# Turning queries and keys with VectorE and the sync queue in place of TensorE

## The reference, cut to what matters

```python
q = (_rmsnorm(c_q, q_norm_g) @ w_uq).reshape(Bsz, S, MLA_H, MLA_QK)
...
dq = _rope(_rmsnorm(d_q.reshape(Bsz, S, DIL_H, DIL_HD), dil_q_g[l]), positions)
dk = _rope(_rmsnorm(d_k.reshape(Bsz, S, DIL_H, DIL_HD), dil_k_g[l]), positions)
y_d = _dilated_attention(dq, dk, d_v.reshape(Bsz, S, DIL_H, DIL_HD)) * jax.nn.silu(g_d)
y = jnp.concatenate([y_a, y_b, y_c, y_d], axis=-1).astype(x.dtype)
x = x + y @ w_out[l]
```

## Time and profile before

| | us |
|---|---|
| three timed runs | 823.65, 824.35, 824.37 |
| median | 824.35 |
| the profiled execution | 823.59 |
| its span, first to last instruction | 821.61 |
| PE busy | 816.4 (99%) |
| VectorE busy | 625.2 (76%) |
| ScalarE busy | 478.2 (58%) |

### The profile page before, as it was taken

How to read it: one execution, slowest core, us unless ns; L and a number is a source line. 1 busy time by engine, 2 the same in 40 slices (tenths; PEclk the granted TensorE clock), 3 DMA queues, 4 the chain that set the end, 5 groups by cost and what they waited for, 6 DMA issues and landing times.

```text
span 821.6 us, 11397 instructions
## 1 busy us (share of the span) xinstructions
PE 816.4 (99%) x4244; PEld 693.0 (84%) x4244; DVE 625.2 (76%) x1118; ACT 478.2 (58%) x788; POOL 54.1 (7%) x64
## 2 busy tenths in 40 slices
PE   9999999999999999999999999999999999999998
PEld 5888888999888888888888888889998888888886
DVE  6678799876886986678965977979769868965542
ACT  6665534777865566433556464357697665654341
POOL 7200000200200000000000000002012000000000
PEclk9999999999999999999999999999999999999999
DMA  9956634566654445655576655457657433456653
GB/s 333 352 204 211 192 129 153 145 208 180 208 176 154 129 132 201 191 191 187 177 253 184 200 161 169 129 147 200 191 173 220 164 129 129 158 177 210 196 189 119
DMA packets 47607, 150.98 MB, mean 184 GB/s; under 512 B 5504, under 2 KB 6192, under 8 KB 47552
## 3 DMA queue, kind: packets, MB, share of 16 engines
q1 hardware_dynamic: 47040, 149.98, 57.0%
q10 hardware_dynamic: 320, 0.21, 0.1%
q0 software_dynamic: 192, 0.07, 0.1%
HBM read 148.13 MB, written 2.11 MB: 183 GB/s over the span
## 4 chain that ended last, share of the span: by engine, by line
PE 91%; DVE 7%; issue 2%; DMA 1%; SPq 0%; ACT 0%; DVEq 0%
PE gemm L665 26%; PE gemm L674 26%; PE gemm L666 26%; DVE arena L1323 3%; DVE w_lo L1354 2%; PE pairs L857 1%; PE pairs L846 1%; PE pairs L833 1%; PE pairs L838 1%; PE pairs L834 1%; PE pairs L795 1%; PE pairs L731 1%; DVE arena L1433 1%; PE pairs L872 1%; DMA u<-in_xT_dram 1%
## 5 line engine op out<-in xcount | busy, mean ns | idle before, releaser
L1354 DVE TENSOR_TENSOR w_lo<-raw,w_hi 128x1024 fp32r<-128x1024 f32 (+2 forms) x295 | 324.7, 1110 | 144.4 <-ACT w_hi L997 142.9
L665 PE MATMUL gemm<-w_hi,a_hi 128*128 128x512 f32 (+1 forms) x1144 | 421.6, 374 | 0.0
L666 PE MATMUL gemm<-w_hi,a_lo 128*128 128x512 f32 (+1 forms) x1144 | 414.4, 368 | 0.0
L997 ACT ACTIVATE w_hi<-raw 128x1024 fp32r<-128x1024 f32 (+2 forms) x295 | 281.0, 967 | 191.4 <-PE gemm L674 136.1
L674 PE MATMUL gemm<-w_lo,a_hi 128*128 128x512 f32 (+1 forms) x1144 | 281.8, 368 | 0.3
L665 PEld LDWEIGHTS gemm<-w_hi,a_hi 128*128 128x128 f32 x1144 | 215.2, 188 | 35.6 <-issue 1.3
L666 PEld LDWEIGHTS gemm<-w_hi,a_lo 128*128 128x128 f32 x1144 | 215.3, 188 | 33.0
L674 PEld LDWEIGHTS gemm<-w_lo,a_hi 128*128 128x128 f32 x1144 | 203.2, 188 | 36.6 <-DVE w_lo L1354 2.0
L573 POOL TENSOR_TENSOR st<-st,powers 128x4 f32<-128x4 f32 (+2 forms) x8 | 8.6, 1074 | 431.5 <-ACT arena L1075 213.4
L1195 ACT ACTIVATE arena<-arena,st 128x128 f32<-128x128 f32 (+1 forms) x32 | 13.1, 444 | 35.4 <-DVE st L1616 35.4
L1027 ACT ACTIVATE u<-gemm,st 128x512 f32<-128x512 f32 (+1 forms) x40 | 22.1, 605 | 18.8 <-PE gemm L674 18.8
(11 more groups left out here) (200 smaller groups left out, 639.0 us busy)
## 6 DMA issues: line engine op xcount, KB each, us to landing
raw<-in_weights_dram SPq DMA_DIRECT2D x225, 512.0 KB, 4.1
raw<-in_weights_dram SPq DMA_DIRECT2D x64, 278.0 KB, 3.1
raw<-in_weights_dram SPq DMA_DIRECT2D x6, 384.0 KB, 3.4
x<-in_x_dram SPq DMA_DIRECT2D x4, 512.0 KB, 6.2
o<-ssd_rows SPq DMA_DIRECT2D x8, 256.0 KB, 4.9
param_rows<-in_params_dram SPq DMA_DIRECT2D x2, 904.0 KB, 7.1
u<-in_xT_dram SPq DMA_DIRECT2D x3, 512.0 KB, 8.1
out_dram<-x SPq DMA_DIRECT2D x3, 512.0 KB, 6.4
```

What stands on the lines that cost most here:

```text
L665: pe.matmul(acc_t[t], a_hi[:, k, tok[t]], hi, start=k == 0, stop=False)
L666: pe.matmul(acc_t[t], a_lo[:, k, tok[t]], hi, start=False, stop=False)
L997: A_(w_hi[:, g % SPLIT, 0:c], raw[:, g % RAW, 0:c], ACT.Copy).then_inc(hi_done, 1)
L1354: TT(w_lo[:, g % SPLIT, 0:c], raw[:, g % RAW, 0:c], w_hi[:, g % SPLIT, 0:c].bitcast(F32), ALU.subtract).then_inc(split_done, 1)
```

## The change

Four of the five jobs leave PE and PSUM; `mla rT` stays. In their place each of the four turns has three steps. `turn_squares` on DVE transposes squares of 32x32 in place of their partitions, 128 partitions at a time, in two instructions of 512 elements, into a buffer (`fold`, for the dilated keys a piece of the arena). The sync queue then moves the squares across the partitions in 16 DMAs of 32 partitions by 256 elements from SBUF to SBUF (`across`). ACT copies the result into the layout that the scores read, as it did from PSUM. `HEADS_AT` gives for each turn the unit of the DVE step, of the DMAs and of the copy. Added waits: SP for the squares; ACT for the DMAs; DVE, ahead of a turn, for the DMAs of the turn before that used the same buffer; and `y_turn` now waits for the copy `dil kT` in place of PE's `mla rT`. `y_turn` starts one unit later.

```diff
-          "mla kv 1": KV_AT, "ssd Y": 76, "ssd yb": 81, "mla qT": 85, "mla kT": 86, "mla rT": 87, "mla S 0": 89, "mla PT 0": 92,
-          "mla S 1": 93, "mla O 0": 94, "dil qT": 95, "mla PT 1": 96, "dil kT": 97, "mla O 1": 98, "dil S 0": 99,
+          "mla kv 1": KV_AT, "ssd Y": 76, "ssd yb": 81, "mla rT": 87, "mla S 0": 89, "mla PT 0": 92,
+          "mla S 1": 93, "mla O 0": 94, "mla PT 1": 96, "mla O 1": 98, "dil S 0": 99,
...
-Y_TURN = {1: 97, 0: 101}
+Y_TURN = {1: 98, 0: 102}
...
+        SQUARES = {"mla q": A(3072, 1024), "mla k": A(4096, 1024), "dil q": u[:, 0, 0:1024], "dil k": u[:, 1, 0:1024]}
+        FOLD = {"mla q": fold, "mla k": fold, "dil q": fold, "dil k": A(6656, 1024)}
+
+        HEADS_AT = {"mla q": (79, 84, 86), "mla k": (85, 90, 88), "dil q": (90, 95, 94), "dil k": (92, 97, 96)}
...
+            def across(to, source, arrived):
+
+                for i in range(4):
+                    for f in range(4):
+                        sp.dma_start(to[32 * f:32 * f + 32, i * S:(i + 1) * S], source[32 * i:32 * i + 32, f * S:(f + 1) * S]).then_inc(arrived, 16)
...
+                    for name in HEADS_AT:
+                        if n == HEADS_AT[name][1]:
+                            sp.wait_ge(*reached("dve", l)(f"{name} squares"))
+                            across(SQUARES[name], FOLD[name], squares_in[name])
...
                 def heads_T(name, dst):
-                    act_.wait_ge(*pe(name))
-                    A_(dst, pair_of(name).rearrange("p b (k s) -> p (b k) s", k=2), ACT.Copy).then_inc(*signal("act", name))
+
+                    act_.wait_ge(squares_in[name], 16 * 16 * (l + 1))
+                    act_.wait_ge(*dve("mla rope" if name[:3] == "mla" else "dil rope 1"))
+                    A_(dst.rearrange("p h (t i a) -> p i (h t) a", t=T, i=4), SQUARES[name].rearrange("p (i c a) -> p i c a", i=4, a=32), ACT.Copy).then_inc(*signal("act", name + "T"))
...
+            def turn_squares(to, rows):
+
+
+                to = to.rearrange("p (f k t a) -> p t k f a", f=4, k=4, t=T)
+                for t in range(T):
+                    last = v.transpose(to[:, t], rows[:, t].rearrange("p k (f b) -> p k f b", f=4))
+                return last
...
                     v.wait_ge(*me(f"y {j}"))
-                    v.wait_ge(*pe("mla rT"))
+
+                    v.wait_ge(*act("dil kT"))
...
+                def head_squares(name):
+
+                    m, i = name[:3], "qk".index(name[4])
+                    if name == "mla k":
+                        v.wait_ge(squares_in["mla q"], 16 * 16 * (l + 1))
+                    if name == "mla q" and l:
+                        v.wait_ge(squares_in["dil q"], 16 * 16 * l)
+                    if name == "dil q":
+                        v.wait_ge(squares_in["mla k"], 16 * 16 * (l + 1))
+                    v.wait_ge(*me(f"mla n {i} 1" if m == "mla" else f"dil rope {i}"))
+                    heads = (mqk if m == "mla" else dqk)[:, :, 4 * i:4 * i + 4, 0:P]
+                    turn_squares(FOLD[name], heads).then_inc(*sig(f"{name} squares"))
```

More of the change, by code:

```diff
@@ L230 @@
         "gla level 6, gla level 7, gla out, ssd cum, ssd gcol, ssd CB, ssd xs, "
-        "mla cT, ssd Y, ssd yb, mla qT, mla kT, mla rT, "
-        "mla S 0, mla PT 0, mla S 1, mla O 0, dil qT, mla PT 1, dil kT, mla O 1, dil S 0, dil PT 0, dil S 1, dil O 0, "
+        "mla cT, ssd Y, ssd yb, mla rT, "
+        "mla S 0, mla PT 0, mla S 1, mla O 0, mla PT 1, mla O 1, dil S 0, dil PT 0, dil S 1, dil O 0, "
         "dil PT 1, dil O 1, yT 2, yT 3",
@@ L239 @@
         "evac 8, mla kv 0, mla kv 1, mla rs 1 sum, dil rs 0 sum, evac 9, dil rs 1 sum, ssd y, mla qT, mla kT, evac 10, "
-        "mla rT, mla P 0, ssd rs sum, mla PT 0, mla P 1, evac 11, dil qT, mla PT 1, dil kT, dil P 0, dil PT 0, "
+        "mla rT, mla P 0, dil qT, ssd rs sum, mla PT 0, dil kT, mla P 1, evac 11, mla PT 1, dil P 0, dil PT 0, "
         "evac 12, dil P 1, dil PT 1, yT 0, yT 1, yT 2, evac 13, yT 3",
@@ L247 @@
         "conv 0 3, conv 0 4, conv 0 5, ssd CB, mla cn, ssd E 0, ssd xdt, mla cT, ssd E 1, ssd M 0, ssd M 1, "
-        "mla n 0 0, mla n 0 1, ssd yT, mla n 1 0, mla n 1 1, mla rope products, mla rope, dil n 0 0, dil n 0 1, "
-        "dil n 1 0, dil n 1 1, dil rope 0 products, dil rope 0, dil rope 1 products, dil rope 1, mla max 0, "
[1 row of a table removed]
+        "mla n 0 0, mla n 0 1, ssd yT, mla q squares, mla n 1 0, mla n 1 1, mla rope products, mla rope, mla k squares, dil n 0 0, dil n 0 1, "
+        "dil n 1 0, dil n 1 1, dil rope 0 products, dil rope 0, dil q squares, dil rope 1 products, dil rope 1, dil k squares, mla max 0, "
[1 row of a table added]
         "dil nmax 0, dil P 0, y turn 0, dil max 1, dil nmax 1, dil P 1, dil ri 0, dil O 0, y 2, yT 0, dil ri 1, dil O 1, yT 1, "
@@ L303, in build @@
         eps, minus_half, log_scale = powers[:, 0:8], powers[:, 8:16], powers[:, 16:17]
+        fold = sb("fold", [P, S * 4])
         st = sb("st", [P, 161])
@@ L428, in build @@
         warm = sem("warm")
+        squares_in = {name: sem(name.replace(" ", "_") + "_squares_in") for name in HEADS_AT}
         setup_chain = sem("setup_chain")
@@ L886, in values, with mla_rT @@
                     last.then_inc(*signal("pe", f"{m} O {i}"))
[L888 removed]
+                def mla_rT():
                     pe.wait_ge(*dve("mla rope"))
[L890 to L895 removed]
                     rr = mrr.rearrange("p t (a b) d -> p t a (b d)", b=2)
@@ L900, in _ @@
                        "gla out": gla_out, "ssd xs": ssd_xs, "ssd cum": ssd_cum, "ssd gcol": ssd_gcol, "ssd CB": ssd_CB, "ssd Y": ssd_Y, "ssd yb": ssd_yb, "mla cT": mla_cT,
-                       "mla qT": mla_qT, "mla kT": mla_kT, "mla rT": mla_rT}
+                       "mla rT": mla_rT}
                 def stages(n):
@@ L1183, in head_sums, with mla_rT @@
                     last.then_inc(*signal("act", f"{m} rs {i} sum"))
+                def mla_rT():
+                    act_.wait_ge(*pe("mla rT"))
+                    A_(mrT.rearrange("p a b s -> p (a b) s"), pair_of("mla rT").rearrange("p b (k s) -> p (b k) s", k=2), ACT.Copy).then_inc(*signal("act", "mla rT"))
                 def heads_T(name, dst):
-                    act_.wait_ge(*pe(name))
-                    A_(dst, pair_of(name).rearrange("p b (k s) -> p (b k) s", k=2), ACT.Copy).then_inc(*signal("act", name))
+                    act_.wait_ge(squares_in[name], 16 * 16 * (l + 1))
+                    act_.wait_ge(*dve("mla rope" if name[:3] == "mla" else "dil rope 1"))
+                    A_(dst.rearrange("p h (t i a) -> p i (h t) a", t=T, i=4), SQUARES[name].rearrange("p (i c a) -> p i c a", i=4, a=32), ACT.Copy).then_inc(*signal("act", name + "T"))
                 def probs(m, i):
@@ L1277, in _ @@
                         ssd_y()
-                    if n == slot("mla qT"):
-                        heads_T("mla qT", mqT)
-                    if n == slot("mla kT"):
-                        heads_T("mla kT", mkT)
+                    for name, to in (("mla q", mqT), ("mla k", mkT), ("dil q", dqT), ("dil k", dkT)):
+                        if n == HEADS_AT[name][2]:
+                            heads_T(name, to)
                     if n == slot("mla rT"):
-                        heads_T("mla rT", mrT.rearrange("p a b s -> p (a b) s"))
-                    if n == slot("dil qT"):
-                        heads_T("dil qT", dqT)
-                    if n == slot("dil kT"):
-                        heads_T("dil kT", dkT)
+                        mla_rT()
                     for m in ("mla", "dil"):
@@ L1728, in _ @@
                             head_norm("mla", 1, t)
+                    for name in HEADS_AT:
+                        if n == HEADS_AT[name][0]:
+                            head_squares(name)
                     if n == 83:
```

13 lines of the change are left out of this document (1 added, 12 removed), and 2 rows, old and new, of the table ORDER.

## The result

The changed kernel takes 854.45 us (median, 853.73 to 856.01) against 824.17 (823.65 to 824.37): 1.037 times as long, 95% interval 1.0357 to 1.0383. The forecast was slower, 830.4 us, range 821 to 842. The sign is right, the size is not: 30.3 us were lost where 6 were forecast.

What follows compares the result with a forecast made beforehand. PE was taken as the bound, busy 816.4 of 821.6 us. With all saved jobs included, late feeders make PE leave each layer's stretch 3.4 us later: 823.6 + 6.8 = 830.4 us, range 821 to 842.

Steps and rivals of the forecast that it cites:

- TensorE's saving, 7.2 us: On PE, two turning jobs per attention go, eight in all at 0.9 us each: 7.2 us.
- PE busy falling to about 809: Sign expected in the profile after: PE's busy time, 816.4 us before, falls to about 809.
- VectorE's turn, 0.70 us an instruction: On VectorE, each turn is two 128x512 transposes at 0.70 us: 1.4 us a turn, 5.6 per layer.
- ScalarE's copy, 1.0: On ScalarE, four copies stay, now from SBUF, priced at 1.0 us each; nothing saved or added.
- Then 16 pieces hold SP for 7.6 us: On the sync queue, each turn's 16 DMAs at 0.47 us hold it 7.6 us; the last lands after 9.1.
- The bounds, 0.37 and 0.69: Lowest and highest price in us of one piece's turn on the sync queue; 0.47 was taken.
- the rival of the full queue: Sync queue fills, a piece takes 0.69 us, four runs in one chain: 13 us more per layer, 856; chance 0.14.
- First knot: At the MLA scores, ScalarE's keys' copy waits until 240.9; PE waits 4.3 us and is 2.5 later than today.
- PE wants that two thirds through unit 85 ... so nothing is lost yet: Before the MLA scores, block 85's low part is ready at 228.8, PE wants it at 231.5: no loss.
- Second knot: At the dilated attention, keys land at 268.6, VectorE is 5.8 us late, PE leaves 3.4 us later per layer.
- The rule that the time to initiate a DMA is usually small: Skill rule for the sync queue: by it the pieces would hide and PE's gain stay; the forecast disagreed for small pieces.
- all hidden: Rival: the pieces and VectorE's turns hide altogether, the full 7.2 us stay: 816.4; chance 0.08.

Runs made afterwards that it cites:

- gpsimd_copies_later: Changed kernel with the 16 pieces a turn issued by GpSimd's queue and ScalarE's two key copies later in its order: 821.64 us.
- pieces from memory: Changed kernel with each of the 16 pieces a turn read from device memory; the squares themselves don't arrive: 835.06 us.
- the tail: Kernel before the change with runs of DMAs of several shapes issued behind its last store, nothing beside them; its time is not compared.
- both queues: Changed kernel with eight pieces of each turn on the sync queue, eight on GpSimd's, and ScalarE's two key copies later: 820.19 us.
- one_dma: Changed kernel with each turn's 16 pieces as one DMA of 128x1024, rows not moved across: 818.74 us.
- two_queues: Changed kernel with eight pieces of each turn on the sync queue and eight on GpSimd's, copies not moved: 823.09 us.

## Why the prediction was wrong, point by point

- **TensorE's saving, 7.2 us: right.** With the waits gone PE is busy 809.6 us (gpsimd_copies_later) against 816.4: 6.8. In the changed kernel itself it is 819.3: the forecast "PE busy falling to about 809" failed because it has no term for the clock. The span grew by 31.1 us: 28.2 more of standing (33.4 against 5.2), 6.8 less of work, and 9.7 (819.3 - 809.6) that the same matmuls took longer at the lower clock. How much of the 9.7 cost time, and how much lay in later waits, was tried for one stretch of four only.
- **VectorE's turn, 0.70 us an instruction: right.** 688 ns, below. ScalarE's copy, 1.0: 1053 ns with 32-element runs, as the rounding of that size.

```profile
L1340 DVE STREAM_TRANSPOSE fold<-u 128x512 f32<-128x512 f32 x12 | 7.8, 688 | 0.0
L1201 ACT ACTIVATE arena<-arena 128x1024 f32<-128x1024 f32 x4 | 4.2, 1053 | 22.1 <-DMA arena<-fold 22.1
```

- **"Then 16 pieces hold SP for 7.6 us": the step that failed.** Measured 10.0 to 10.8. I chose 0.47 "since it is the same behind a load of 128 x 1280 numbers ... and so does not follow the size". That it doesn't follow the size is true. But both rows were loads from device memory, and a piece comes from a place on the chip: 0.46 against 0.63. The bounds, 0.37 and 0.69, held it; the value was taken from the wrong kind, and no row of the kernel before shows a DMA between two places on the chip. The landing was 1.9 us for 2.0. With the right kind of source put back to 0.46 us, 19.4 of the 24.1 us of the miss were gone.
- **Why 0.16 us a piece weigh 19 us.** 2.6 us a run, four runs a layer, each of which starts when the one before is through and its held block is split: 8 x 2.6 = 21. The traces bear this out: from the start of the first run to the end of the fourth, the first layer takes 63.8 us in the changed kernel (215.51 to 279.35) and 53.8 with pieces from memory (216.06 to 269.86), 10 us more. I had this chain in the rival of the full queue (0.69 us, 856 us, chance 0.14), with the wrong reason: in the tail, too, a piece took 0.63 with nothing large outstanding. That its 856 came so near is luck in part: with the measured price the same sum gives 830.4 + 21 = 851, and the 0.06 us that it had too much stands in for the 4.7 us that have other causes.
- **First knot: mechanism right.** The copy of the keys stood from 235.6 to 246.7 and blocks 89 and 90 behind it, as described. At the priced piece TensorE waited 1.7 + 2.8 = 4.5 us there, for 4.3 forecast. I had the keys' copy in hand as what holds the rest up, and didn't see that moving the two key copies would take away over a third of the loss.
- **"PE wants that two thirds through unit 85 ... so nothing is lost yet": wrong at the measured hold.** Block 85 landed at 230.4 and not 226.6; TensorE waited 1.4 us for it (until 231.50).
- **Second knot: right in place, short in size.** The dilated keys landed at 280.6 (forecast 268.6), their copy held the probabilities (L1209) and the rounding of unit 97, so that VectorE came to its low part only at 284.45 (forecast about 272.4). TensorE waits for VectorE's taps at L891 even with both queues, 2.4 us in all. I put this down to the move of the turns of y and to VectorE's added turns, which was not tried; it would be most of what separates 820.2 from 816.4.
- **The rule that the time to initiate a DMA is usually small** (the Trainium skill, the page and section above): it doesn't hold for this shape. A piece took the queue 0.63 us and landed 1.9 us after its issue, a third; a DMA sixteen times as large took 0.47 and landed after 4.9 in one_dma, a tenth. The other rule of the Trainium skill, "DMA: Bandwidth & Descriptors", Rules for kernel authors, that DMAs under 64 KB are mostly overhead, agrees with the tail: 8 KB and 32 KB cost the same turn. But so did 128 KB there, so these runs don't show that bound.
- **The lower end.** With few issues the change was worth 5.2 us (818.74), near the rival "all hidden" at 816.4. What stood between was the count of DMAs; that kernel doesn't move the rows across.

## What to carry to other kernels

Price a run of small DMAs as count times the queue's turn, from rows with the same kind of source, and set that against what the loads queued behind it have in store. Here a hold of 2.5 us a run was as good as free, one of 5 us cost half a microsecond a run, and from 7.4 to 10 us nearly every microsecond counted (19.4 us for eight runs of 2.6 more). An engine's wait for a late transfer belongs as late in its order as its reader allows, behind all work that is ready. And where a term multiplies by 128 issues, its uncertainty makes the range, not the value that looked nearest.

## What the runs showed of the hardware

- The sync queue's turn was 0.63 us for a DMA from place to place on the chip, back to back, for 8 KB to 128 KB (8x1024: 0.68), and 0.44 to 0.47 from device memory, for 32 KB and 512 KB; ScalarE's queue needed the same 0.64 on the chip (10.25 / 16). A single one of 512 KB on the chip took 0.47 (one_dma).
- GpSimd's queue was the faster one for these pieces, 0.49 us, but they landed later: 3.4 us (median, arena) against 1.9. This need not be the queue: there the weight blocks moved beside them, and with both queues at work the sync queue's pieces took 3.5 too (arena, median, two_queues).
- One DMA of 512 KB on the chip, beside the weights, landed 4.9 us after its issue, the median of four:

```profile
arena<-fold SPq DMA_DIRECT2D x4, 512.0 KB, 4.9
```

- After four waits of 2.2 to 5.9 us TensorE's granted clock was 0.50 for 3 to 7 us; behind two others, of 3.1 and 2.35 us in the second layer, it stayed at full speed. In the one place tried, the low clock lay in the shadow of the next wait.
